# Dense weights of the second token tile: one factor of 13 groups built ahead, both factors of the other 19 compared in 16 bit

## What is computed

```python
v1, i1 = lax.top_k(s1, 16); v2, i2 = lax.top_k(s2, 16)      # 8 heads, 128 keys a side
sv, si = lax.top_k(v1[..., :, None] + v2[..., None, :], 16)  # of 16 x 16 pairs
e = i1 * 128 + i2                                            # at the chosen pairs
a = gelu(einsum('nhkd,nd->nhk', u[e], hx))
y = einsum('nhk,nhkd->nd', softmax(sv) * a, v[e])
```

## Time and profile before

| what | value |
|---|---|
| median of 3 runs | 1351.16 us |
| the profiled execution's own time | 1357.94 us |
| its span, first to last instruction | 1356.1 us |
| busy: TensorE, VectorE, ScalarE, GpSimd | 1100.9, 967.6, 308.5, 670.9 us |
| mean granted clock of TensorE | 0.89 |
| bytes moved by the DMA | 460.64 MB, mean 340 GB/s |

### The profile page before, as it was taken

The page is one execution under the profiler, slowest core; times in us unless marked ns, Lnnn a source line. Parts: engine busy times, 40 slices in busy tenths (PEclk is TensorE's granted clock), DMA queues, the critical chain, the costliest instruction groups (busy, mean ns, idle before and its releaser), DMA issues. The chain is left out here.

```text
span 1356.1 us, 13047 instructions
## 1 busy us (share of the span) xinstructions
PE 1100.9 (81%) x4321; PEld 733.4 (54%) x4321; DVE 967.6 (71%) x2135; ACT 308.5 (23%) x844; POOL 670.9 (49%) x570
## 2 busy tenths in 40 slices
PE   6898898996677378667566743779999999999998
PEld 3444583443344377325346732656666666666665
DVE  2631069999778589948888997998865666666666
ACT  2142122222311132121354464970000000000000
POOL 2110036557375455545665566565574454444452
PEclk9889899998798589786678865779999999999999
DMA  9975569969999979989998888779999999999998
GB/s 332 341 297 207 206 232 359 350 217 365 343 357 383 366 275 378 385 326 324 331 367 300 307 282 289 234 224 394 405 409 409 410 409 409 409 409 409 410 406 324
DMA packets 167348, 460.64 MB, mean 340 GB/s; under 512 B 14912, under 2 KB 36848, under 8 KB 167024
## 3 DMA queue, kind: packets, MB, share of 16 engines
q0 software_dynamic: 74784, 271.66, 53.7%
q1 hardware_dynamic: 92496, 188.14, 37.3%
HBM read 453.41 MB, written 6.34 MB: 339 GB/s over the span
## 5 line engine op out<-in xcount | busy, mean ns | idle before, releaser
L704 POOL DMA_INDIRECT rows_ring<-in_peer_u,expert x384 | 498.5, 1298 | 388.7 <-DVE dots L1716 286.5
L1716 DVE CUSTOM_DVE_ANT_0 rows_ring<-rows_ring,arena 128x1024 f32<-128x1024 f32 x384 | 458.6, 1223 | 99.5 <-DMA rows_ring<-in_peer_u,expert 96.5
L1337 PE MATMUL wide<-ring,arena 128*128 128x512 f32 x1024 | 441.6, 594 | 0.7 <-issue 0.7
L1337 PEld LDWEIGHTS wide<-ring,arena 128*128 128x128 f32 x1024 | 302.4, 295 | 139.5 <-issue 3.5
L1721 DVE SCALAR_TENSOR_TENSOR x<-rows_ring,dots,x 128x1024 f32<-128x1024 f32 x128 | 164.4, 1284 | 96.3 <-DMA rows_ring<-in_peer_v,expert 95.8
L704 POOL DMA_INDIRECT rows_ring<-in_peer_v,expert x128 | 128.6, 1005 | 135.2 <-DVE x L1721 123.6
L1015 PE MATMUL transB<-ident,arena 128*128 128x128 f32 x165 | 32.9, 329 | 48.5 <-DMA arena<-in_cache_a_k 18.5
L1015 PEld LDWEIGHTS transB<-ident,arena 128*128 128x128 f32 x165 | 22.1, 165 | 57.3 <-ACT arena L737 20.7
L1322 PE MATMUL accumA<-arena,hot 128*128 128x128 f32 x128 | 23.9, 345 | 34.6 <-issue 23.6
L737 ACT ACTIVATE arena<-transB 128x512 f32<-128x512 f32 (+2 forms) x44 | 24.7, 565 | 115.2 <-PE transB L1015 95.2
L1040 PE MATMUL accumA<-ring,arena 128*128 128x512 f32 (+1 forms) x96 | 41.4, 591 | 4.7 <-DMA ring<-in_w_in 3.5
(11 more groups left out here) (304 smaller groups left out, 1441.8 us busy)
## 6 DMA issues: line engine op xcount, KB each, us to landing
ring<-in_peer_v SPq DMA_DIRECT2D x128, 512.0 KB, 6.8
arena<-in_w_in SPq DMA_DIRECT2D x15, 2048.0 KB, 15.1
ring<-in_w_in SPq DMA_DIRECT2D x9, 2048.0 KB
arena<-in_w_pq SPq DMA_DIRECT2D x7, 2048.0 KB, 14.1
ring<-in_w_pq SPq DMA_DIRECT2D x5, 2048.0 KB
arena<-in_w_out SPq DMA_DIRECT2D x4, 2048.0 KB, 10.5
arena<-in_w_br_a SPq DMA_DIRECT2D x3, 2048.0 KB, 9.7
ring<-in_w_br_b SPq DMA_DIRECT2D x3, 2048.0 KB
```

What stands on the lines that cost most here:

```text
L704: pool.indirect_dma_start(rowbuf[:, n % ROWS, :], None, u_rows if n < U_ROWS else v_rows, index).then_inc(S(f"rows{n % ROWS}"), 16)
L1337: return pe.matmul(wide[:, 2 * t + half, :], dense[t][:, :, b], vblock[:, b % VBLOCKS, half * 512:half * 512 + 512], start=b == 0, stop=b ...
L1716: v.tensor_tensor_reduce(row, row, h2[:, t, :], 1.0, 0.0, ALU.mult, ALU.add, dots[:, t, k:k + 1]).then_inc(S("row_used"), 1)
```

## The change

Tile 1's groups are split. Thirteen of them (`EARLY`, the even ones from 0 to 24) get their `hot2` ahead: TensorE transposes tile 1's keys at unit 47 (`keys_ahead`), ScalarE copies them and makes the 13 sets at units 48 to 63 (`one_hots_ahead`) in parts of the arena that will hold tile 1's dense weights for the tokens that are put last (`HELD`). Their `hot1` is made by VectorE as before. The other 19 (`LATER`, the odd ones to 23, and 25 to 31) are made as tile 0's are. Tile 1's weights are due at unit 64 instead of 65, its transposition at 64, its first group at 64.5, and there are six groups to a unit. `both`, `places4` and `keys16` move to other places and exist for each tile: tile 1's `both` is the fourth buffer of the block ring, so SyncE loads the fourth block when all groups are built. Tile 0's keys are narrowed straight from PSUM.

```diff
-DENSE = [(35, 44, 1.8), (64.5, 65, 4)]
+DENSE = [(35, 44, 1.8), (64, 64.5, 6)]
 
 
 ORDER = [[28, 29, 30, 31] + list(range(4, 8)) + list(range(12, 20)) + list(range(4)) + list(range(8, 12)) + [20, 21, 27] + list(range(22, 27)),
-         list(range(TGROUPS))]
+         []]
+
+
+AHEAD = [22528, 23040, 23552, 24064, 25600, 30208, 18944, 19456, 19968, 20480, 20992, 21504, 22016]
+AHEAD_AT = [48, 49.5, 51, 52, 53.5, 55, 56.5, 57.5, 58.5, 61, 61.5, 62.5, 63]
+EARLY = [2 * n for n in range(len(AHEAD))]
+LATER = [g for g in range(TGROUPS) if g not in EARLY]
+HELD = [(a - BLOCKS * P) // (TOKENS * P) for a in AHEAD]
+ORDER[1] = [n for n in range(TGROUPS) if n not in HELD] + HELD
...
-        both = part(22528, 1024).bitcast(BF16).rearrange("p (s a k t) -> p s a k t", s=2, a=2, t=TOKENS)
-        places4 = part(23552, 256).bitcast(BF16).rearrange("p (k t) -> p k t", t=TOKENS)
-        keys16 = part(23808, 128).bitcast(BF16).rearrange("p (a n) -> p a n", a=2)
+        both = [a.bitcast(BF16).rearrange("p (s a k t) -> p s a k t", s=2, a=2, t=TOKENS)
+                for a in (part(16384, 1024), ring0[:, 3072:4096])]
+        places4 = [a.bitcast(BF16).rearrange("p (k t) -> p k t", t=TOKENS)
+                   for a in (tables[:, 0:256], cT[:, :, :].rearrange("p a n -> p (a n)"))]
+        keys16 = [a.bitcast(BF16).rearrange("p (a n) -> p a n", a=2)
+                  for a in (own[:, :], new_bias[:, :, :].rearrange("p h k -> p (h k)"))]
+
+        def hot2_of(t, g):
+
+            if t and g in EARLY:
+                return part(AHEAD[EARLY.index(g)], TOKENS * P)
+            return hot2[:, (LATER.index(g) if t else g) % 2, :]
...
             for b in range(BLOCKS):
                 if b >= VBLOCKS:
                     sp.wait_ge(S("block_used"), b - VBLOCKS + 1)
+                elif b == VBLOCKS - 1:
+                    sp.wait_ge(S("built"), 2 * TGROUPS)
                 sp.dma_start(vblock[:, b % VBLOCKS, :], i["peer_v"][0, b * P:b * P + P, :]).then_inc(
...
-                act.activation(turned[:, 1, :], bank[:, 1, :], ACT.Copy, scale=-1.0 if t else 1.0).then_inc(
-                    S("turned_copied"), 1)
-                act.activation(turned[:, 0::2, :], bank[:, 0::2, :], ACT.Copy).then_inc(S("turned_copied"), 1)
+                if t:
+                    act.activation(turned[:, 2, :], bank[:, 2, :], ACT.Copy).then_inc(S("turned_copied"), 1)
+                else:
+                    act.wait_ge(to(C, "logits_read"), 1)
+                    act.activation(turned[:, 2, :], bank[:, 2, :], ACT.Copy).then_inc(S("turned_copied"), 1)
+                    act.activation(keys16[0], bank[:, 0:2, :], ACT.Copy).then_inc(S("turned_copied"), 1)
...
-                if t == 0:
-                    yield DENSE[0][1] - 1
-                    act.wait_ge(S("turned_copied"), 2)
-                    act.wait_ge(to(C, "transposed"), batch(C, "prob", 1, PAIRS - 1) + 1)
-                    act.activation(keys16, turned[:, 0:2, :], ACT.Copy).then_inc(S("keys16_ready"), 1)
...
-                        act.wait_ge(S("turned_copied"), 4)
-                        act.wait_ge(S("iota_set"), 1)
-                    if n >= 2:
-                        act.wait_ge(S("built"), n - 1)
-                    if t == 0:
-                        act.wait_ge(S("compared"), g + 1)
-                        act.activation(chunks(hot2[:, g % 2, :], TOKENS), both[:, g % 2, 1].rearrange("p k t -> p t k"),
-                                       ACT.Copy).then_inc(S("hot2_ready"), 1)
-                    for j, tok in enumerate(tokens_of(t, g)):
-                        if t:
-                            act.activation(hot2[:, n % 2, j * P:j * P + P], iota[:, :], ACT.Abs,
-                                           bias=turned[:, 1, tok:tok + 1]).then_inc(S("apart"), 1)
-                        else:
-                            ins = act.activation(hot1[0][:, g % 2, j * P:j * P + P], both[:, g % 2, 0, :, j], ACT.Copy,
+                        act.wait_ge(S("turned_copied"), 3)
+                    if t == 0 or g in LATER:
+                        m = LATER.index(g) if t else g
+                        act.wait_ge(S(f"compared{t}"), m + 1)
+                        if t == 0 and g >= 2:
+                            act.wait_ge(S("built"), g - 1)
+                        elif t:
+                            act.wait_ge(S("built"), max(n - 1, TGROUPS))
+                            if m >= 2:
+                                act.wait_ge(S("built"), TGROUPS + LATER[m - 2] + 1)
+                        act.activation(chunks(hot2_of(t, g), TOKENS), both[t][:, m % 2, 1].rearrange("p k t -> p t k"),
+                                       ACT.Copy).then_inc(S(f"hot2_ready{t}"), 1)
+                        for j, tok in enumerate(tokens_of(t, g)):
+                            ins = act.activation(hot1[t][:, n % 2, j * P:j * P + P], both[t][:, m % 2, 0, :, j], ACT.Copy,
                                                  scale=turned[:, 2, tok:tok + 1])
-                    if t:
-                        act.wait_ge(S("apart"), TOKENS * (g + 1))
-                        act.activation(hot2[:, n % 2, :], hot2[:, n % 2, :], ACT.Relu, bias=1.0, scale=-1.0).then_inc(
-                            S("hot2_ready"), 1)
-                    else:
-                        ins.then_inc(S("hot1_ready0"), 1)
+                        ins.then_inc(S(f"hot1_ready{t}"), 1)
                     if g:
                         put(g - 1)
                 put(TGROUPS - 1)
...
+            def one_hots_ahead():
+
+                yield AHEAD_AT[0] - 0.5
+                act.wait_ge(S("ahead_turned"), 1)
+                act.activation(turned[:, 1, :], sumB[:, P:2 * P], ACT.Copy, scale=-1.0).then_inc(S("ahead_copied"), 1)
+                act.activation(turned[:, 0, :], sumB[:, 0:P], ACT.Copy).then_inc(S("ahead_copied"), 1)
+                act.wait_ge(to(C, "logits_read"), 1)
+                act.activation(keys16[1], chunks(sumB[:, 0:2 * P], 2), ACT.Copy).then_inc(S("ahead_copied"), 1)
+                for k, g in enumerate(EARLY):
+                    yield AHEAD_AT[k]
+                    if k == 0:
+                        act.wait_ge(S("ahead_copied"), 1)
+                        act.wait_ge(S("iota_set"), 1)
+                        act.wait_ge(to(C, "transposed"), batch(C, "prob", 1, PAIRS - 1) + 1)
+                    elif k == AHEAD.index(25600):
+                        act.wait_ge(to(C, "pair_scored"), 2 * PAIRS)
+                    elif k == AHEAD.index(18944):
+                        act.wait_ge(S("state_stored"), 16 * 15)
+                        act.wait_ge(to(C, "out_done"), 2)
+                    elif k == AHEAD.index(20480):
+                        act.wait_ge(S("picked"), 4 * SAMPLE + 2)
+                    dst = hot2_of(1, g)
+                    for j, tok in enumerate(tokens_of(1, g)):
+                        act.activation(dst[:, j * P:j * P + P], iota[:, :], ACT.Abs,
+                                       bias=turned[:, 1, tok:tok + 1]).then_inc(S("apart"), 1)
+                    act.wait_ge(S("apart"), TOKENS * (k + 1))
+                    act.activation(dst, dst, ACT.Relu, bias=1.0, scale=-1.0).then_inc(S("ahead_ready"), 1)
...
                 for n, src in enumerate((keys[:, t, :, 0], keys[:, t, :, 1], dots[:, t, :])):
-                    ins = pe.transpose(built[0][:, n * P:n * P + P], src, ident[:, :])
+                    if t == 0 or n == 2:
+                        ins = pe.transpose(built[0][:, n * P:n * P + P], src, ident[:, :])
                 ins.then_inc(S("turned"), 1)
...
-                    pe.wait_ge(S("hot2_ready"), n + 1)
-                    pe.wait_ge(S(f"hot1_ready{t}"), g + 1)
+                    if t and g in EARLY:
+                        pe.wait_ge(S("ahead_ready"), EARLY.index(g) + 1)
+                        pe.wait_ge(S("weighted"), EARLY.index(g) + 1)
+                    else:
+                        m = LATER.index(g) if t else g
+                        pe.wait_ge(S(f"hot2_ready{t}"), m + 1)
+                        pe.wait_ge(S(f"hot1_ready{t}"), m + 1)
                     if g == 1:
-                        pe.wait_ge(S("turned_copied"), 2 * t + 2)
+                        pe.wait_ge(S("turned_copied"), t + 2)
                     elif n >= 2:
                         pe.wait_ge(S("dense_put"), n - 1)
                     for j in range(TOKENS):
-                        ins = pe.matmul(built[(g + 1) % 2][:, j * P:j * P + P], hot2[:, n % 2, j * P:j * P + P],
+                        ins = pe.matmul(built[(g + 1) % 2][:, j * P:j * P + P], hot2_of(t, g)[:, j * P:j * P + P],
                                         hot1[t][:, n % 2, j * P:j * P + P], start=True, stop=True)
...
+            def keys_ahead():
+
+                yield AHEAD_AT[0] - 1
+                pe.wait_ge(S("routed"), 8)
+                pe.wait_ge(to(C, "attended"), 2)
+                for n in range(2):
```

(64 more changed lines are left out.)

## The result

The changed kernel takes 1364.26 us (median of 8 runs, 1355.52 to 1367.59) against 1350.93 us of the kernel before (8 runs, 1347.51 to 1359.33): a ratio of 1.0082, 95% interval 1.0052 to 1.0113. It is slower by 0.8%; the forecast was 1361, in a range from 1344 to 1371. A ratio here is worked out over the single runs; it is not the quotient of the two medians and differs from it by up to 0.2%, so where the two say different things both are given.

A forecast was written before the change was run, and what follows sets the result against it. Bound: block product and gathered rows sharing a full DMA, 1.30 us per transfer. Earlier product -5.0, fewer rows +12.4, fourth block +1.3, sets ahead +1, tile 0 0: +9.7 on the 1351.2 median gives 1361 us, range 1344 to 1371.

The forecast's parts named there:

- What bounds the kernel: Last third: block product and gathered rows share the DMA and end together; each 512 KB transfer there costs 1.30 us.
- Work of a group: Tile 1's groups: 13 early and 19 others cost ScalarE 49.4 us, VectorE 51.3 with rows; work alone some 55 us.
- The wait that it adds: In a pair of groups, ScalarE's copy of the odd group's own result waits for TensorE's four products, delaying the next widening.
- VectorE's coupling: In tile 1's phase, VectorE's rows and comparisons delay ScalarE about 1 us four times, adding some 4 us.
- Sum of the phase: Tile 1's weight building: 69.5 us at the fast clock, 81.5 at the slow, 75.9 taken; product 5.0 us earlier.
- rival A: Fast TensorE clock throughout tile 1's phase: product at 896.5, about 1353 us by the median; chance 0.25.
- Rows done by then: Rows gathered before the block product starts: 286.5, 9.5 fewer than before, costing 12.4 us.
- One-hots ahead: ScalarE's 13 sets before unit 64, some 25 us of work, delay the kernel 0 to 5 us; 1 taken.
- The sum: Whole kernel: all terms together + 9.7 us, added to the median of 1351.2, giving 1361 us.
- The 1.3 us of the fourth block: Before the block product, 3 blocks instead of 4 are loaded ahead: + 1.3 us, without TensorE waiting.
- B: Slow clock in tile 1's phase, or sets ahead hold VectorE up: 1365 to 1370 us; chance 0.18.
- C: TensorE's latency hidden in tile 1's phase: phase 55.4 us, 11 us less, 1340 by the median; chance 0.15.

## Why the prediction was right

**What bounds the kernel** held, and all else rests on it. The price of a transfer during the product came out at 1.305 us against 1.30 forecast, rows remaining 225 against 225.5, the rows' end 456.7 us after the product's start against 456.0, and the block product's end 14 us before it as forecast (1335.6 and 1349.7).

**Work of a group** held: early comparisons 1.11 us, 16-bit ones 0.61, widening 0.57, weighting 1.19.

**The wait that it adds** held to 0.03 us: 3.60 and 4.52 us for a pair against 3.63 and 4.55, and 2.75 when the experiment took the wait away. The 3.63 and 4.55, in the forecast's sum as 43.6 and 54.6 for 12 pairs, are an estimate that no run shows as it stands: ScalarE's chain for a pair with 1.16 or 2.08 us for TensorE's four products. Windows of the kernel before over the two products, with the columns of the earlier trace rows, have them at granted clocks of 0.50 and 1.00:

```profile
838.90:841.00 2.10, 2.07 (x8) 1.77 (x8) 1.96 (x6) 2.07 (x6) 1.74 (x2) 0.50 0.57 224
843.50:844.70 1.20, 1.16 (x8) 0.97 (x8) 1.20 (x4) 1.20 (x4) 1.16 (x1) 1.00 0.90 253
```

VectorE's coupling was taken at some 4 us in four places; ScalarE waited 3.7 us, 4 times, for a comparison:

```profile
ACT hot L995 <- DVE ring L1756: 3.7, 4, 1.5
```

**Sum of the phase**: 72.8 us against 75.9. The form was right and the clock's share off: 8 of 12 pairs ran at the fast level (the odd group's products in 1.13 us), not the 47% taken, and 72.8 lies between the forecast's 69.5 and 81.5. TensorE was granted 0.78 on average, against 0.72 before; as the same kernel had 0.75 and 0.69 in two profiles, these 3 us may be chance. For rival A I had counted on pairs that keep TensorE busier; it was busy 43.9 of 72.8 us, 60%, less than the 69% of before (52.7 of 76.2). That a busier TensorE is granted the faster clock was my estimate, and no run shows it: before, the phase with 69% had 0.72, the changed one with 60% had 0.78.

**Rows done by then**: 9.5 fewer forecast, 9 fewer measured (287 against 296). The experiment with four groups per unit shows the price: with 10 rows back the kernel was 14 us faster.

**One-hots ahead** is the term that was mis-sized. I took 1 us, between 0 and 5, on the ground that a later wait for rows takes up most of a delay; it is 5 to 6 by the stretch of the profiles (216.6 against 211.3) and by the runs with unused sets, if roughly. The waits for rows stayed as they were. The start of the phase shows it too: forecast 4.6 us earlier, it came 219.5 us after the division in both kernels.

**The sum**: the product started 3.5 us earlier against the division step, not 5.0, being 3.1 us better in the phase and 4 to 5 worse ahead of it. The two errors nearly cancelled, which was luck: the rows end 10.8 us later than in the kernel before by the profiles; the ratio gives + 11, the medians + 13, and + 9.7 was forecast. The 1.3 us of the fourth block were not measured by themselves; TensorE's idle time ahead of the product's instructions sums to 0.8 us, 0.7 before, so it waited for no block.

**Rivals.** A (fast clock, +2) and B (+14 and more) lie on either side of what came. C needed a phase under 67.3 us; the experiment without the wait had 60.3 and came out level with the kernel before, since 5 us of sets and its 27 rows stand against it. By my estimate C's 55 us of phase and 11 us gained would thus have been too much by the price of the sets.

## What to carry to other kernels

Where one in-order engine both feeds a long stage and does the work that frees a transfer ring, shortening the stage is no gain by itself: count how many transfers fit into it, and what each costs later, when the DMA is full (here 9 rows fewer, at 1.30 us each while it moves 407 to 409 GB/s). Two kinds of groups that alternate break the spacing by which one engine's copy had been hidden behind the next group's work, so write out one pair of the new order with each wait before adding up busy times (here 3.60 us at the fast clock, and 2.75 with the copy one set later). And an engine at less than half load (in the kernel before, ScalarE was busy 88.4 of the 217.5 us from the division to tile 1's weights) is no free place for 24 us of work if another waits for it in order; here that cost about a fourth of what was put there, some 6 us.

## What the runs showed that I had not expected

- TensorE's clock doesn't keep still in the phase. In the kernel before, products of 1.16 us every 2.31 us, with pauses of at most 1.16 us (the prediction has them well under 1 us each), gave way five times to products of 1.97 to 2.08 us, and the mean granted clock was 0.72. Without the wait in a pair the clock was 0.78 to 0.84 (four profiles), in the nine others 0.69 to 0.78. The changed kernel had 0.78 with pauses of up to 3.2 us, but 0.70 with four groups per unit, so pairs by themselves don't give a faster clock; what does was not tried.
- Nearly the same code reaches the same step at 599 to 617 us in thirteen profiles, a scatter of 18 us. It is about as wide as that of the times themselves (the kernel before ran from 1341 to 1361 us beside one set of experiments). What makes it was not looked into.
- The same row had two prices: 1.30 us of the DMA while that was full (407 to 409 GB/s, DMA share 1.02 to 1.03), and only VectorE's 1.15 us in the phase, where at 186 to 280 GB/s the rows came as fast as VectorE used them (0.3 us of waiting for rows in the changed kernel's phase, at most 0.8 in any of the thirteen).
